# A hybrid decoder step on one core: peer_u handed over in a second layout, and the gates read four blocks at a time

## The chip, the cores and the metric

The kernel runs on one core of one Trainium2 chip. The number is the device time of one execution in microseconds. A core has five engines that work side by side and meet at semaphores: TensorE (PE), VectorE (DVE), ScalarE (ACT), GpSimd (POOL) and SyncE (SP, which here only issues transfers). Sixteen DMA engines move the data between memory, SBUF and back; one queue is fed by SP, another by GpSimd.

## What is computed

One decoder layer for 512 prompt tokens and 32 sample tokens, with a model dimension of 2048, in fp32. A pooling and gating mixer and a memory attention come first. The last sublayer, PEER, is what the change touches: every token picks 16 of 16384 experts in each of 8 heads, and each expert is one row of `peer_u` and one row of `peer_v`.

```python
def block(xb):
    q = (xb @ peer_wq).reshape(PEER_BLOCK, PEER_HEADS, 2, PEER_HALF)
    s = jnp.einsum('thpd,pkd->thpk', q, peer_subkeys).astype(jnp.float32)
    sv, si = lax.top_k(s, PEER_TOPK)
...
    fv, fi = lax.top_k(cand, PEER_TOPK)
    eidx = jnp.take_along_axis(cidx, fi, axis=-1)
    gate = jax.nn.softmax(fv, axis=-1).astype(xb.dtype)
    act = jax.nn.gelu(jnp.einsum('thkd,td->thk', peer_u[eidx], xb))
    return jnp.einsum('thk,thkd->td', gate * act, peer_v[eidx])
```

## The kernel before, in words

**Two ways through PEER.** 384 prompt tokens (N) go densely: their product with all 16384 rows of `u`, a GELU, the product with a mostly zero gate matrix, and the product with all rows of `v`. The other 128 prompt tokens and the 32 sample tokens go sparsely: GpSimd gathers their expert rows with 320 indirect transfers of 1 MB into seven buffers (`gbuf`), and VectorE does one "step" for each.

**Three passes of fp32r.** Each fp32 operand is split in a high half (a copy to fp32r on ScalarE) and a low half (the difference, on VectorE), and each product is made of three matmuls: high by high, high by low, low by high.

**The column stage.** The rows of `u` are cut in 128 blocks of 128 experts. One block is a "column" for PE: 16 chunks of the model dimension, three matmuls of 128x384 each, 48 in all, into a bank of `pl` (L1127). The model dimension must lie on partitions for it, and in memory a row of `u` lies along a partition. So during column b PE also transposes block b+1 from `u_raw`: after the second chunk of each four, four transposes (`turn_rows`, L1095) into a bank of `pp`. ScalarE copies the bank to `ut_hi` (`rows_hi`, L1418), VectorE makes `ut_lo` (`rows_lo`, L1838). `u_raw`, `ut_hi` and `ut_lo` have two slots. SP reloads half a slot of `u_raw` once PE has transposed it (`t_done`). After its column a block's GELU goes to `fg` (L1424).

**What runs beside the columns.** In the first 32 columns (PICK) VectorE and GpSimd pick the experts: `half_list` and `pick`, with calls of `next_rows` between the operations, which keep up the low halves of `u`. VectorE's instructions stand in one fixed order, so a call that waits holds the pick. The softmax's exponential stands on ScalarE between two columns. Then PE turns `ij` and `gw` to `ijt` (L1160), and 24 columns follow that also build the gate matrices (`gate_columns`): for every four tokens VectorE compares an iota with the picked indices (`one_hot`, L1886 and L1887), PE multiplies (L1104), ScalarE copies to `gs` (L1436), and GpSimd's queue stores to `g_scr`.

**Ahead and steady.** The gates are there only after these columns, so the GELUs of the first 60 blocks (AHEAD) are stored in `s_scr`. From block 60 on each column multiplies its own GELU by its gate (`gated`, L1931) and one of those stored (`ahead_gated`, L1936), and SP stores both to `p_scr`. SP's order in a steady column is: first half of `u_raw`, store of `sa`, store of `fg`, second half of `u_raw`, load of this block's gate `gt`, a wait until the store of `sa` has landed, loads of the next `sa` and its gate `ga`. A gate load reads 64 floats (256 bytes) at a time, 768 runs for a block. VectorE's gather steps start at column 62 (STEP_COL), three in two columns.

**The value stage.** 256 half blocks of `v` with their `p`, 24 matmuls each (L1186), again with high and low halves (L1490, L1493, L1940, L1944) and gather steps between.

Of the kernel before, what the change touches and what calls it, by code (L numbers as in the profile page):

```python
# [24 lines left out]
P = 128  # L25
# [25 lines left out]
PICK = 32  # L51
AHEAD = 60
STEP_COL = 62
STEP_M = 246
GELU_S = 43
# [21 lines left out]
def program(nc, a, o):  # L77
    ctx = ExitStack()
    with ctx:
# [400 lines left out]
        gt = at("gt", TMP, [P, 2, N])  # L480
        sa = at("sa", TMP + 3072, [P, 2, N])
        ga = at("ga", TMP + 9728, [P, 2, N])
# [3 lines left out]
        t_done, t_hi, t_lo = sem("t_done"), sem("t_hi"), sem("t_lo")  # L486
        u_done, ge_done, gm_done = sem("u_done"), sem("ge_done"), sem("gm_done")
        f_stored = [sem("f_stored0"), sem("f_stored1")]
        g_in, pa_stored = [[sem(f"{w}{s}") for s in range(2)] for w in ("g_in", "pa_stored")]
# [4 lines left out]
        def gates_in(b):  # L494
            n = (b - AHEAD) // 2 + 1
            return 48 * n if b < 2 * AHEAD else 16 * n + 32 * (AHEAD // 2)

# [11 lines left out]
        def acc_bank(c):  # L509

            k = c % 8
            return (pt[k] if k < 2 else pp[k // 2 - 1][:, k % 2] if k < 6 else pl[:, k % 2])[:, 0:N]
# [59 lines left out]
        def _(sp):  # L572
# [60 lines left out]
            uv = a["peer_u"][0].rearrange("(b p) d -> b p d", p=P)  # L633
            vv = a["peer_v"][0].rearrange("(b p) (s d) -> s b p d", p=P, s=2)
            gv = g_scr.rearrange("h p i t -> i p h t")

            def u_load(i, d, h, free=None):

                if free is not None:
                    sp.wait_ge(t_done, free)  # L640
                sp.dma_start(u_raw[:, d, h * HD:(h + 1) * HD], uv[i * 2 + d][:, h * HD:(h + 1) * HD])\
                    .then_inc(u_in[d][h], 16)

            def next_u(i, d, h):

                u_load(i + 1, d, h, i * 8 + (4 * d + 2 * (h + 1)))
# [5 lines left out]
            def p_store(i, d):  # L652
                sp.wait_ge(gm_done, i * 4 + (2 * d + 1 - 2 * AHEAD) if not isinstance(i, int) else gated_count(i * 2 + d))
                sp.dma_start(p_scr[i * 2 + d], fg[:, d, :]).then_inc(f_stored[d], 16)

            def g_load(i, d):
                sp.dma_start(gt[:, d, :].rearrange("p (h t) -> p h t", t=HALF), gv[i * 2 + d]).then_inc(g_in[d], 16)

            def ahead_load(i, d, first=False):
                if not first:  # L660
                    sp.wait_ge(pa_stored[d], i * 16)
                sp.dma_start(sa[:, d, :], s_scr[i * 2 + d]).then_inc(g_in[d], 16)
                sp.dma_start(ga[:, d, :].rearrange("p (h t) -> p h t", t=HALF), gv[i * 2 + d]).then_inc(g_in[d], 16)

            def ahead_store(i, d):
                sp.wait_ge(gm_done, i * 4 + (2 * d + 2))
                sp.dma_start(p_scr[i * 2 + d], sa[:, d, :]).then_inc(pa_stored[d], 16)
# [31 lines left out]
            def steady_body(i, d, first=False):  # L699
                b = i * 2 + d if isinstance(i, int) else None  # L700
                if b is None or b + 2 < NK:
                    next_u(i, d, 0)
# [4 lines left out]
                if b is None or AHEAD + 2 <= b < 2 * AHEAD + 2:  # L707
                    ahead_store(i - AHEAD // 2 - 1, d)
                if b is None or b >= AHEAD + 2:
                    p_store(i - 1, d)  # L710
                if b is None or b + 2 < NK:
                    next_u(i, d, 1)
                g_load(i, d)
                if b is None or b < 2 * AHEAD:
                    if b == AHEAD or b == AHEAD + 1:
                        sp.wait_ge(f_stored[d], 16 * AHEAD // 2)
                    ahead_load(i - AHEAD // 2, d, b is not None and b < AHEAD + 2)
            for d in range(2):
                steady_body(AHEAD // 2, d)
            with sp.Fori(AHEAD // 2 + 1, AHEAD) as i:  # L720
                for d in range(2):
                    steady_body(i, d)
            for b in range(2 * AHEAD, NK):
                if b == NK - 2:
                    for s in range(2):
                        sp.wait_ge(pa_stored[s], 16 * AHEAD // 2)
                    for d in range(4):
                        p_load(0, d)
                    sp.wait_ge(t_done, 4 * (NK - 1))
                    for d in range(2):  # L730
                        v_load(0, 0, d)
                steady_body(b // 2, b % 2)
            sp.wait_ge(t_done, 4 * NK)
            for d in range(2, 4):
                v_load(0, 0, d)
            for d in range(2):
                p_store(NK // 2 - 1, d)
# [29 lines left out]
        def _(pe):  # L767
# [317 lines left out]
            def turn_rows(i, d, g, dst, first=False):  # L1085

                if g % 2 == 0:
                    pe.wait_ge(u_in[d][g // 2], i * 16 + 16)
                if first:
                    if g >= 2:  # L1090
                        pe.wait_ge(t_lo, g - 1)
                else:
                    pe.wait_ge(t_lo, i * 8 + (4 * d + g - 3))
                for c in range(4):
                    last = turn(dst[:, c * P:(c + 1) * P], u_raw[:, d, (4 * g + c) * P:(4 * g + c + 1) * P], ident[:, :])  # L1095
                last.then_inc(t_done, 1)

# [1114 lines left out]
```

## Time and profile before

| What | Value |
|---|---|
| Median of 3 runs | 4282.88 us (4282.53 to 4288.63) |
| Profiled execution | 4279.69 us, span 4278.0 us |
| PE busy | 4077.9 us, 95% of the span |
| DVE busy | 2592.4 us, 61% |
| ACT busy | 1390.0 us, 32% |
| POOL busy | 714.2 us, 17% |
| Moved by DMA | 943.10 MB, mean 220 GB/s |
| Mean granted TensorE clock | 0.977 |

Busy times are averages over stages that differ: the projections up to about 1757 us, the column stage from there to 3165 us, the value stage to about 4238 us, then the last norms. Matmuls overlap in the pipe, so the mean duration of one is longer than the distance from one start to the next. A DMA share of 1 says that the sixteen engines had packets in flight all the time. What is named as idle or waiting on an engine costs time only where nothing else ends later.

### The profile page before, as it was taken

What the parts mean: (1) busy time and instruction counts of PE and PEld (TensorE: products, weight loads), DVE (VectorE), ACT (ScalarE), POOL (GpSimd) and SP (SyncE); (2) the same over time, 40 slices, a digit from 0 to 9 for tenths busy, and PEclk for the clock granted to TensorE, in tenths of its full rate; (3) what the DMA queues carried; (4) which work ended last, traced back from release to release, by engine and by line L of the source; (5) the groups of instructions that cost most, each with busy time, mean ns of one, the idle gap of its engine ahead of it and who ended that gap; (6) DMA issues with size and microseconds to landing.
All of it is one profiled execution on the core that took longest, in us unless ns stands there. A gap on an engine that the chain in (4) does not pass through costs nothing.

```text
span 4278.0 us, 69824 instructions
## 1 busy us (share of the span) xinstructions
PE 4077.9 (95%) x26191; PEld 3935.2 (92%) x26191; DVE 2592.4 (61%) x4092; ACT 1390.0 (32%) x1876; POOL 714.2 (17%) x514
## 2 busy tenths in 40 slices
PE   8998979979889979999999999999999999999996
PEld 6788969979849979999999999999999999999996
DVE  3324232351453266666477556666679899898896
ACT  3433221132442132222355422222233333333333
POOL 0000020020000030044100001111123333344430
PEclk9989989989999999999999999999999999999998
DMA  6542222213542212233344599999999999999994
GB/s 224 196 117 55 82 59 79 78 50 118 197 138 79 78 54 77 97 117 121 113 171 169 195 315 355 354 350 355 355 339 403 397 411 409 394 400 396 402 384 135
DMA packets 495289, 943.10 MB, mean 220 GB/s; under 512 B 126372, under 2 KB 375904, under 8 KB 443032
## 3 DMA queue, kind: packets, MB, share of 16 engines
q1 hardware_dynamic: 443552, 567.36, 39.8%
q0 software_dynamic: 51616, 374.19, 21.8%
q8 instruction: 68, 1.11, 0.1%
q14 instruction: 53, 0.43, 0.0%
HBM read 866.63 MB, written 73.56 MB: 220 GB/s over the span
## 4 chain that ended last, share of the span: by engine, by line
PE 91%; DVE 4%; DMA 2%; ACT 2%; DVEq 1%; issue 1%; POOL 0%; SPq 0%; ACTq 0%
PE pl L1127 25%; PE pp L197 24%; PE pp L1186 12%; PE pt L1186 6%; PE pl L1186 6%; PE pp L1095 5%; PE pt L1104 2%; PE pp L792 2%; PE pt L792 1%; PE pl L792 1%; PE pp L859 1%; DMA kv<-in_cache_mem_k 1%; DMA raw<-in_w_mk 1%; PE pl L821 1%; PE pt L823 1%; PE pl L1046 1%
## 5 line engine op out<-in xcount | busy, mean ns | idle before, releaser
L1127 PE MATMUL pl<-h_hi,ut_hi 128*128 128x384 f32 x2048 | 734.7, 359 | 0.6 <-ACT ijt L1465 0.6
L1127 PE MATMUL pl<-h_hi,ut_lo 128*128 128x384 f32 x2048 | 692.1, 338 | 0.0
L1127 PE MATMUL pl<-h_lo,ut_hi 128*128 128x384 f32 x2048 | 691.3, 338 | 0.0
L1838 DVE TENSOR_TENSOR ut_lo<-pp,ut_hi 128x512 fp32r<-128x512 f32 x508 | 350.2, 690 | 483.3 <-ACT ut_hi L1418 479.1
L1418 ACT ACTIVATE ut_hi<-pp 128x512 fp32r<-128x512 f32 x508 | 304.1, 599 | 820.6 <-PE pp L1095 763.4
L212 DVE TENSOR_TENSOR w_lo<-raw,w_hi 128x2048 fp32r<-128x2048 f32 x120 | 274.8, 2291 | 424.0 <-ACT w_hi L207 424.0
L1490 ACT ACTIVATE v_hi<-v_raw 128x1024 fp32r<-128x1024 f32 x256 | 271.9, 1062 | 682.6 <-PE pl L1186 438.3
L1940 DVE TENSOR_TENSOR v_lo<-v_raw,v_hi 128x1024 fp32r<-128x1024 f32 x256 | 313.2, 1223 | 123.3 <-ACT v_hi L1490 122.6
L1127 PEld LDWEIGHTS pl<-h_lo,ut_hi 128*128 128x128 f32 x2048 | 387.1, 189 | 0.0
L1127 PEld LDWEIGHTS pl<-h_hi,ut_hi 128*128 128x128 f32 x2048 | 386.2, 189 | 0.8 <-ACT ijt L1465 0.8
L1127 PEld LDWEIGHTS pl<-h_hi,ut_lo 128*128 128x128 f32 x2048 | 384.7, 188 | 0.0
L207 ACT ACTIVATE w_hi<-raw 128x2048 fp32r<-128x2048 f32 x120 | 229.4, 1911 | 418.9 <-PE pp L197 298.2
L197 PE MATMUL pp<-h_hi,w_hi 128*128 128x272 f32 x1664 | 350.9, 292 | 9.4 <-DVE w_lo L212 8.3
L197 PE MATMUL pp<-h_hi,w_lo 128*128 128x272 f32 x1664 | 347.9, 291 | 0.0
L197 PE MATMUL pp<-h_lo,w_hi 128*128 128x272 f32 x1664 | 346.6, 290 | 0.0
L1186 PE MATMUL pp<-p_hi,v_hi 128*128 128x384 f32 x1024 | 344.6, 336 | 0.0
L1186 PE MATMUL pp<-p_hi,v_lo 128*128 128x384 f32 x1024 | 343.8, 336 | 0.0
L1186 PE MATMUL pp<-p_lo,v_hi 128*128 128x384 f32 x1024 | 342.9, 335 | 0.0
L1095 PE MATMUL pp<-ident,u_raw 128*128 128x128 f32 x2032 | 304.4, 272 | 0.0
L2175 POOL DMA_INDIRECT gbuf<-in_peer_v,eix x128 | 242.6, 1895 | 355.6 <-DVE xr L1924 323.0
L1924 DVE SCALAR_TENSOR_TENSOR xr<-gbuf,wr,xr 128x2048 f32<-128x2048 f32 x128 | 300.4, 2347 | 0.1
L1920 DVE SCALAR_TENSOR_TENSOR gbuf<-gbuf,xr 128x2048 f32<-128x2048 f32 x128 | 292.2, 2283 | 0.0
(387 smaller groups left out, 8257.7 us busy)
## 6 DMA issues: line engine op xcount, KB each, us to landing
u_raw<-in_peer_u SPq DMA_DIRECT2D x256, 512.0 KB
v_raw<-in_peer_v SPq DMA_DIRECT2D x256, 512.0 KB
p_f<-p_scr SPq DMA_DIRECT2D x256, 192.0 KB
raw<-in_w_in SPq DMA_DIRECT2D x24, 1024.0 KB, 5.6
g_scr<-gs POOLq DMA_DIRECT2D x6, 4096.0 KB, 13.6
raw<-in_w_mk SPq DMA_DIRECT2D x16, 1024.0 KB, 4.9
raw<-in_w_mv SPq DMA_DIRECT2D x16, 1024.0 KB, 4.8
raw<-in_w_out SPq DMA_DIRECT2D x16, 1024.0 KB, 5.9
```

The lines of the kernel that those rows point to most:

```text
L197: last = nc.tensor.matmul(pp[s][:, b, 0:t1 - t0], w[:, s, k, :], x[:, k, t0:t1], start=(k == 0 and w is w_hi and x is x_hi), stop=(k == KC ...
L212: nc.vector.tensor_tensor(w_lo[:, s], raw[:, s], w_hi[:, s].bitcast(F32), ALU.subtract).then_inc(lo_ready, 1)
L1095: last = turn(dst[:, c * P:(c + 1) * P], u_raw[:, d, (4 * g + c) * P:(4 * g + c + 1) * P], ident[:, :])
L1127: last = mm(pl[:, d, 0:N], w[:, d, k, :], x[:, k, S:S + N], start=(k == 0 and w is ut_hi and x is h_hi), stop=(k == KC - 1 and w is ut_lo))
L1186: last = mm(acc_bank(c), w[:, d, c * P:(c + 1) * P], x[:, d, :], start=(b == 0 and w is v_hi and x is p_hi), stop=(b == NK - 1 and w is v_lo))
L1418: f(ut_hi[:, d, 4 * g:4 * g + 4, :], src.rearrange("p (c i) -> p c i", c=4), ACT.Copy).then_inc(t_hi, 1)
L1490: f(v_hi[:, d, :], v_raw[:, d, :], ACT.Copy).then_inc(hi_done, 1)
L1838: tt(ut_lo[:, d, 4 * g:4 * g + 4, :], src.rearrange("p (c i) -> p c i", c=4), ut_hi[:, d, 4 * g:4 * g + 4, :].bitcast(F32), ALU.subtract). ...
L1920: ins = stt(row, row, 1.0, x, ALU.mult, ALU.mult, accum_out=s[:, k:k + 1])
L1924: ins = stt(x, row, w[:, k:k + 1], x, ALU.mult, ALU.add)
L1940: tt(v_lo[:, m % 4, :], v_raw[:, m % 4, :], v_hi[:, m % 4, :].bitcast(F32), ALU.subtract).then_inc(lo_done, 1)
L2175: g.indirect_dma_start(gbuf[n % NG_BUF][:, :], None, rows, bass.IndirectOffsetOnAxis(ix, 0))\
```

## The change

1. `peer_u` is handed over a second time, laid out as [block, model dimension within a chunk, chunk, expert]. The dense path loads its blocks from that; the gathers keep the old one. `turn_rows` is gone, and `u_raw` holds what was in the banks.
2. `rows_hi` and `rows_lo` read `u_raw` in SBUF, half a block (128x1024) at a time, two pieces a block instead of four. SP reloads half a slot when the low half has been made (`t_lo`).
3. Gates are read for four blocks at once (`gate_fours`), 1024 bytes at a time, in two buffers each for the current and the stored blocks (`g4`, `a4`).
4. `one_hot` makes three operations of 128x4x128 with broadcast operands instead of eight of 128x128, and works one group ahead of PE.
5. PICK is 28 instead of 32, AHEAD 56 instead of 60, STEP_COL 58 instead of 62, GELU_S 46 instead of 43. The steps' pace is 5 in 4 columns from 58 and 2 a column from 112, 99 in all before the value stage, as many as before.
6. The columns' accumulators lie in `pp[0]`, and the value stage takes its banks in another order. The last select-scores product moves into column 0, the first block's halves ahead of the last panel's evacuation on ScalarE.
7. On VectorE one score list less stands before the first halves.

```diff
-PICK = 32
-AHEAD = 60
-STEP_COL = 62
+PICK = 28
+AHEAD = 56
+STEP_COL = 58
...
             def u_load(i, d, h, free=None):

                 if free is not None:
-                    sp.wait_ge(t_done, free)
+                    sp.wait_ge(t_lo, free)
...
+            def gate_fours(k, both=True):
+
+                for dst, q in ((g4, k + AHEAD // 4),) + (((a4, k),) if both else ()):
+                    sp.dma_start(dst[k % 2][:, :, :, :], gv[q]).then_inc(g4_in[k % 2], 16)
...
+            def ahead_steady(j, d, b=None):
+
+                s = d % 2
+                sp.wait_ge(t_lo, j * 16 + (2 * d + 1))
+                sp.dma_start(u_raw[:, s, 0:HD], uv[j * 8 + (d + 2)][:, 0:HD]).then_inc(u_in[s][0], 16)
                 if b == AHEAD:
                     s_store(AHEAD // 2 - 1, 1)
-                    for s in range(2):
-                        sp.wait_ge(g_stored[s], 16 * ND)
+                    for x in range(2):
+                        sp.wait_ge(g_stored[x], 16 * ND)
+                    for k in range(2):
+                        gate_fours(k)
                 if b is None or b >= AHEAD + 2:
+                    sp.wait_ge(gm_done, j * 16 + (2 * (d - AHEAD) - 2))
+                    sp.dma_start(p_scr[j * 8 + (d - AHEAD - 2)], sa[:, s, :]).then_inc(pa_stored[s], 16)
+                    sp.wait_ge(gm_done, j * 16 + (2 * (d - AHEAD) - 3))
+                    sp.dma_start(p_scr[j * 8 + (d - 2)], fg[:, s, :]).then_inc(f_stored[s], 16)
+                sp.wait_ge(t_lo, j * 16 + (2 * d + 2))
+                sp.dma_start(u_raw[:, s, HD:D], uv[j * 8 + (d + 2)][:, HD:D]).then_inc(u_in[s][1], 16)
+                if b is None or b >= AHEAD + 2:
+                    sp.wait_ge(pa_stored[s], j * 64 + (16 * (d // 2 - AHEAD // 2)))
...
+                sp.dma_start(sa[:, s, :], s_scr[j * 8 + (d - AHEAD)]).then_inc(s_in[s], 16)
+                if d % 4 == 1 and (b is None or b > AHEAD + 1):
+
+                    x = (d // 4 + 1) % 2
+                    sp.dma_start(g4[x][:, :, :, :], gv[j * 2 + (d // 4 + 1)]).then_inc(g4_in[x], 16)
+                    if b is None or b < 2 * AHEAD - 4:
+                        sp.dma_start(a4[x][:, :, :, :], gv[j * 2 + (d // 4 + 1 - AHEAD // 4)]).then_inc(g4_in[x], 16)
...
                 for k in range(KC):
-                    if k % 4 == 0:
-                        pe.wait_ge(t_lo, i * 8 + (4 * d + k // 4 + 1))
+                    if k % 8 == 0:
+                        pe.wait_ge(t_lo, i * 4 + (2 * d + k // 8 + 1))
                     for w, x in ((ut_hi, h_hi), (ut_hi, h_lo), (ut_lo, h_hi)):
-                        last = mm(pl[:, d, 0:N], w[:, d, k, :], x[:, k, S:S + N],
+                        last = mm(pp[0][:, d, 0:N], w[:, d, k, :], x[:, k, S:S + N],
                                   start=(k == 0 and w is ut_hi and x is h_hi), stop=(k == KC - 1 and w is ut_lo))
                     if k == KC - 1:
                         last.then_inc(u_done, 1)
-                    if k % 4 == 1:
-                        if more:
-                            turn_rows(i + d, 1 - d, k // 4, turn_bank(k // 4))
-                        if gate is not None:
-                            gate_matrix(group(gate, k // 4)[0], k // 4 % 2)
+                    if start and d == 0 and k == 7:
+                        select_scores(NPANEL - 1, 1)
+                    if gate is not None and k % 4 == 1:
+                        gate_matrix(group(gate, k // 4)[0], k // 4 % 2)
...
+            def rows_hi(i, d, h, used=None):
+
+                act.wait_ge(u_in[d][h], i * 16 + 16)
                 if used is not None:
                     act.wait_ge(u_done, used)
-                f(ut_hi[:, d, 4 * g:4 * g + 4, :], src.rearrange("p (c i) -> p c i", c=4), ACT.Copy).then_inc(t_hi, 1)
+                f(ut_hi[:, d, 8 * h:8 * h + 8, :], u_raw[:, d, h * HD:(h + 1) * HD].rearrange("p (c i) -> p c i", c=8),
+                  ACT.Copy).then_inc(t_hi, 1)
...
+            def rows_lo(i, d, h):
+
+                dve.wait_ge(t_hi, i * 4 + (2 * d + h + 1))
+                tt(ut_lo[:, d, 8 * h:8 * h + 8, :], u_raw[:, d, h * HD:(h + 1) * HD].rearrange("p (c i) -> p c i", c=8),
+                   ut_hi[:, d, 8 * h:8 * h + 8, :].bitcast(F32), ALU.subtract).then_inc(t_lo, 1)
...
+                k_all = iota_k[:, :].rearrange("p (x k) -> p x k", x=1).to_broadcast([P, 4, P])
+                tt(oh[:, s, 1, :, :], k_all, of(0), ALU.is_equal)
+                tt(oh[:, s, 0, :, :], k_all, of(1), ALU.is_equal)
+                dve.drain()
+                tt(oh[:, s, 1, :, :], oh[:, s, 1, :, :], of(2), ALU.mult).then_inc(oh_ready, 1)
...
             for b in range(AHEAD, NK):
                 more = b + 1 < NK
-                upto = max(0, b + 1 - STEP_COL) * 3 // 2
...
+                upto = max(0, b + 1 - STEP_COL) * 5 // 4 + max(0, b + 1 - 2 * AHEAD) * 3 // 4
+                if more:
+                    rows_lo((b + 1) // 2, (b + 1) % 2, 0)
+                if b > AHEAD:
+                    gated(b - 1)
+                if AHEAD < b <= 2 * AHEAD:
+                    ahead_gated(b - AHEAD - 1)
+                if more:
+                    rows_lo((b + 1) // 2, (b + 1) % 2, 1)
+                else:
+                    for m in range(2):
+                        v_split(m)
+                        p_split(m)
+                while done[0] < upto:
+                    step()
```

## Rows read from the trace of the kernel before

**Rows 1.** The page's chain that ended last, shares of the span by line.
```profile
PE pl L1127 25%; PE pp L197 24%; PE pp L1186 12%; PE pt L1186 6%; PE pl L1186 6%; PE pp L1095 5%; PE pt L1104 2%; PE pp L792 2%; PE pt L792 1%; PE pl L792 1%; PE pp L859 1%; DMA kv<-in_cache_mem_k 1%; DMA raw<-in_w_mk 1%; PE pl L821 1%; PE pt L823 1%; PE pl L1046 1%
```
**Rows 2.** The page's groups: shapes, count | busy us, mean ns | idle before, releaser.
```profile
L1838 DVE TENSOR_TENSOR ut_lo<-pp,ut_hi 128x512 fp32r<-128x512 f32 x508 | 350.2, 690 | 483.3 <-ACT ut_hi L1418 479.1
L1418 ACT ACTIVATE ut_hi<-pp 128x512 fp32r<-128x512 f32 x508 | 304.1, 599 | 820.6 <-PE pp L1095 763.4
...
L1095 PE MATMUL pp<-ident,u_raw 128*128 128x128 f32 x2032 | 304.4, 272 | 0.0
```
**Rows 3.** Windows: us, busy of PE, PEld, DVE, ACT, POOL, PEclk, DMA share, GB/s.
```profile
1757.00:2095.00 338.00, 336.43 (x2147) 330.04 (x2145) 205.63 (x576) 105.64 (x183) 110.64 (x54) 1.00 0.37 123
...
2431.00:3165.00 734.00, 734.00 (x4611) 723.37 (x4610) 468.66 (x614) 209.90 (x363) 101.20 (x106) 1.00 0.99 343
...
3190.00:3700.00 510.00, 508.23 (x2922) 507.46 (x2920) 457.93 (x430) 182.99 (x249) 175.06 (x111) 1.00 1.02 404
```
**Rows 4.** Timeline of ScalarE, two GELUs two columns apart: start, us, what.
```profile
2800.26 0.49 ACT L1424 ACTIVATE fg<-pl 128x384 f32<-128x384 f32 x1 [0.45 <-PE pl L1127]
...
2820.63 0.49 ACT L1424 ACTIVATE fg<-pl 128x384 f32<-128x384 f32 x1 [0.45 <-PE pl L1127]
```
**Rows 5.** Timeline of PE, first product of the last column and first value product.
```profile
3156.59 0.34 PE L1127 MATMUL pl<-h_hi,ut_hi 128*128 128x384 f32 x1
...
3165.02 0.34 PE L1186 MATMUL pt<-p_hi,v_hi 128*128 128x384 f32 x1
```
**Rows 6.** Timeline of PE in a column that builds gate matrices.
```profile
2134.80 0.60 PE L1095 MATMUL pp<-ident,u_raw 128*128 128x128 f32 x4
2135.23 1.10 PE L1104 MATMUL pt<-oh 128*128 128x128 f32 x8
2136.09 0.42 PE L1127 MATMUL pl<-h_hi,ut_hi 128*128 128x384 f32 x1
```
**Rows 7.** The page's groups of the value stage and of the gather steps.
```profile
L1490 ACT ACTIVATE v_hi<-v_raw 128x1024 fp32r<-128x1024 f32 x256 | 271.9, 1062 | 682.6 <-PE pl L1186 438.3
L1940 DVE TENSOR_TENSOR v_lo<-v_raw,v_hi 128x1024 fp32r<-128x1024 f32 x256 | 313.2, 1223 | 123.3 <-ACT v_hi L1490 122.6
...
L1924 DVE SCALAR_TENSOR_TENSOR xr<-gbuf,wr,xr 128x2048 f32<-128x2048 f32 x128 | 300.4, 2347 | 0.1
```
**Rows 8.** Timeline of VectorE: softmax of the gates, one gate product.
```profile
2073.18 0.82 DVE L1861 TENSOR_TENSOR gw<-gw,sums 128x640 f32<-128x640 f32 x1
2075.12 0.82 DVE L1864 TENSOR_REDUCE sums<-gw 128x40 f32<-128x640 f32 x1 [1.12 <-ACT gw L1460]
...
2599.79 0.54 DVE L1931 TENSOR_TENSOR fg<-fg,gt 128x384 f32<-128x384 f32 x1
```
**Rows 9.** Timelines of VectorE, GpSimd and PE where the pick ends.
```profile
2037.08 2.81 DVE L1816 TENSOR_TENSOR eq<-iota,ab_f 128x2560 f32<-128x2560 f32 x1
...
2051.26 0.47 POOL L2136 TENSOR_TENSOR ij<-eq 128x160 f32<-128x160 f32 x1
...
2094.15 0.55 PE L1160 MATMUL pt<-ident,ij 128*128 128x128 f32 x3 [1.27 <-DVE sums L1878]
...
2097.54 0.69 PE L1127 MATMUL pl<-h_hi,ut_hi 128*128 128x384 f32 x1 [0.58 <-ACT ijt L1465]
```
**Rows 10.** Groups by form of 1810 to 1900 us.
```profile
L1789 DVE MATCH_REPLACE8 cand<-gw,cand 128x256 f32<-128x256 f32 x15 | 6.0, 410 | 0.0
```
**Rows 11.** DMA of 2600 to 2980 us, rates in 40 slices of 9.5 us.
```profile
GB/s 394 327 367 359 345 373 323 376 319 392 318 390 315 388 321 381 347 348 371 340 373 323 380 321 397 311 394 306 390 329 372 353 344 371 342 371 331 379 314 399
DMA packets 92892, 134.83 MB, mean 355 GB/s; under 512 B 61915, under 2 KB 76145, under 8 KB 85617
```
**Rows 12.** Waits of SP's queue, 2600 to 3100 us: us in total, times, longest.
```profile
SPq L662 <- DMA p_scr<-sa: 87.1, 35, 3.8
```
**Rows 13.** Timelines of SP and ScalarE in the value stage.
```profile
3182.85 0.29 SPq L677 DMA_DIRECT2D p_f<-p_scr  x1
...
3190.64 1.06 ACT L1490 ACTIVATE v_hi<-v_raw 128x1024 fp32r<-128x1024 f32 x1 [5.42 <-DMA p_f<-p_scr]
```

More of the change, by code:

```diff
@@ new lines, in _ @@
+            for d in range(8):
+                ahead_steady(AHEAD // 8, d, AHEAD + d)
+            with sp.Fori(AHEAD // 8 + 1, AHEAD // 4 - 1) as j:
+                for d in range(8):
+                    ahead_steady(j, d)
+            for d in range(4):
+                ahead_steady(AHEAD // 4 - 1, d, 2 * AHEAD - 8 + d)
+            for b in range(2 * AHEAD - 4, 2 * AHEAD):
+                ahead_steady(AHEAD // 4 - 1, b % 8, b)
+            for b in range(2 * AHEAD, NK):
+                s = b % 2
+                if b + 2 < NK:
+                    next_u(b // 2, s, 0)
+                if b < 2 * AHEAD + 2:
+                    sp.wait_ge(gm_done, 2 * (b - AHEAD) - 2)
+                    sp.dma_start(p_scr[b - AHEAD - 2], sa[:, s, :]).then_inc(pa_stored[s], 16)
@@ L724, in _ @@
                 if b == NK - 2:
-                    for s in range(2):
-                        sp.wait_ge(pa_stored[s], 16 * AHEAD // 2)
+                    for x in range(2):
+                        sp.wait_ge(pa_stored[x], 16 * AHEAD // 2)
                     for d in range(4):
                         p_load(0, d)
-                    sp.wait_ge(t_done, 4 * (NK - 1))
+                    sp.wait_ge(t_lo, 2 * (NK - 1))
                     for d in range(2):
                         v_load(0, 0, d)
-                steady_body(b // 2, b % 2)
@@ L733, in _ @@
-            sp.wait_ge(t_done, 4 * NK)
+                p_store(b - 2)
+                if b + 2 < NK:
+                    next_u(b // 2, s, 1)
+                if b % 4 == 1 and b + 4 < NK:
+                    gate_fours((b - AHEAD) // 4 + 1, False)
+            sp.wait_ge(t_lo, 2 * NK)
             for d in range(2, 4):
@@ L1083, in _ @@
                     select_scores(i * 2 + (WQ0 + d - 1), (d + 1) % 2)
[L1085 to L1096, printed above, removed]
             def gate_matrix(n, s):
@@ L1423, in gelu, with column @@
                     act.wait_ge(f_stored[d], i * 16)
-                f(fg[:, d, :], pl[:, d, 0:N], ACT.Gelu_apprx_tanh).then_inc(ge_done, 1)
-            def column(i, d, gate=None, more=True):
+                f(fg[:, d, :], pp[0][:, d, 0:N], ACT.Gelu_apprx_tanh).then_inc(ge_done, 1)
+            def column(i, d, gate=None):
                 first = isinstance(i, int) and i == 0 and d == 0
                 for g in range(4):
-                    if more:
-                        rows_hi(i + d, 1 - d, g, turn_bank(g), None if first or g else i * 2 + d)
+                    if g % 2 == 0:
+                        if first:
+                            act.wait_ge(panel_done, NPANEL)
+                        rows_hi(i + d, 1 - d, g // 2, None if first else i * 2 + d)
+                    if first and g == 1:
+                        scores_out(15)
                     if gate is not None:
```

185 lines of the change are left out of this document (68 added, 117 removed).

## The prediction

> **What bounds the kernel now.** Read the chain that ended last first: its longest entries are all TensorE's, 25% in the products of `ut` with `h` (L1127) and 5% in the transposes of `u` (L1095) [rows 1]. The groups give the counts: 2032 transposes (16 more stand before the first column), with two off-path companions, the high half on ScalarE (L1418) and the low half on VectorE (L1838), both of which wait longer than they work [rows 2]. The windows say what else is full: in the column stage PE is busy for 336 of the first 338 us and for all of the last 734, at full granted clock, and in the last part the DMA share is 0.99 as well [rows 3]. So two things are full there, PE and, from about 2450 us, the DMA engines. The reader has to hold both: time taken from PE is only won if the DMA engines can deliver the same bytes sooner.
>
> **What a transpose costs on the path.** Its mean of 272 ns overlaps its neighbours, so I take distances between starts. Two GELUs later in the steady part are 20.37 us apart, 10.19 us a column [rows 4]. The last column has no transposes: its 48 products start at 3156.59 and the next work at 3165.02, 8.43 us, 0.1756 us each [rows 5]. The difference, 1.76 us a column, is the price of 16 transposes, 0.44 us for each group of four. In the columns that also build gate matrices, four transposes start at 2134.80 and the gate matrix at 2135.23, 0.43 us [rows 6]: the same.
>
> **Term 1: no transposes.** 127 columns carry them: 127 x 1.75 = 222 us. The chain's own entry, 5% of 4278 us, gives 214, rounded as it is [rows 1]. Block 0's 16 transposes stand before the first product, at the same price 1.8 us. The select-scores product beside them moves into column 0 and costs what it did. Sum: -224 us.
>
> **Term 2: the halves are made from SBUF in pieces of 1024.** Per column ScalarE did 4 x 0.60 and will do 2 x 1.06 (as `v_hi`, same shape and source); VectorE did 4 x 0.69 and will do 2 x 1.22 (as `v_lo`) [rows 2, 7]. Both drop. They lie behind PE: block b+1 is made while column b runs. If that cover were gone the column would start at least 1.06 + 1.22 = 2.3 us late. In the columns from 58 on VectorE has 2.44 + 2 x 0.55 (gates) + 1.25 x 2.35 (gather steps) = 6.5 us [rows 7, 8] of work in 8.43; from 112 on 2.44 + 0.55 + 2 x 2.35 = 7.7. It stays below PE, tightly at the end, where a half may be late by a step and still be ready, since it is due only 8.4 us after its column's start. Cost 0.
>
> **Term 3: one-hot matrices in three wide operations.** No row has this form. Its neighbours on VectorE: 384 elements took 0.54, 640 with a broadcast operand 0.82, 2560 with two broadcast operands 2.81 us [rows 8, 9]. For 512 that is 0.68, so 2.0 us for three. The upper end is `v_lo` of 1024, 1.22 each, 3.7 us. PE's period for a group becomes 12 x 0.1756 + 0.86 for the gate matrix, 3.0 us [rows 5, 6]; VectorE needs 2.0 + 0.61 for its half of a `ut_lo`, 2.6. I take the lower end, because 384 and 640 enclose 512. It would bind from 0.8 us an operation on. Cost 0, upper value at 0.9 us: (2.7 + 0.07 + 0.61 - 3.0) x 96 groups = 36 us; at the upper end itself, 3.7 + 0.61 - 3.0 = 1.3 us a group, 125 us.
>
> **Term 4: the pick of experts gets 28 columns instead of 32.** Now the last `eq` on VectorE starts at 2037.08, GpSimd ends its reductions at 2051.7, and PE turns `ij` at 2094.15: some 40 us of slack, filled with columns [rows 9]. In the new order the last pick begins with half-blocks 51, 52, 53; the 52nd (block 26) needs column 24 finished. From there, with the rows' durations: GELU and high half 1.7, low half 1.2, the rest of the top-16, fifteen small operations of about 0.41 like the replacement, with one more half 7.1 [rows 10], index work and `eq` 3.6, so `eq` ends 13.6 us after column 25 starts, the subtraction at 14.5. ScalarE stands at the exponential until 16.6 (the reduction now starts 1.94 us after the subtraction did [rows 8]) and only then makes block 27's high halves; VectorE does reduction, reciprocal and product (some 2.2, three operations of the sizes of these rows) and then the low half: 20.1. Column 27 is due at 16.9. So PE waits about 3.3 us, and pays perhaps 1 us of lower clock behind it, as after the present pause, where the first product is 0.69 us long instead of 0.34 [rows 5, 9]. GpSimd, 11.7 us behind the end of `eq`, ends at 25.3, before column 27 does (28.5), so the second pause keeps its present length. +4 us; 0 if the pick runs ahead, 12 if the chain slips by a column.
>
> **Term 5: DMA.** Per column from 58 to 111 the queues carry u 1.05 MB, two stores and one load of 0.197, two gate loads of 0.197 (now 0.79 MB once in four columns) and 1.25 gathers of 1.05: 3.34 MB. The gathers' pace per us is kept (1.5 in 10.19 before, 1.25 in 8.43). In 8.43 us that is 397 GB/s; from 112 on, 3.54 MB, 420 GB/s for 16 columns, part of which the seven gather buffers give from stock. Now the same stage runs at 343 to 355 GB/s with the share at 0.99, which looks full. But 61915 of its 92892 packets are under 512 B, the slices reach 390 to 399 GB/s in columns with two steps, and SP waits only 87.1 / 35 = 2.5 us for a store to land; the value stage keeps 404 GB/s with PE busy for 508 of 510 us [rows 3, 11, 12]. The gates' packets go from 256 to 1024 B, a quarter of the number. So I take cost 0, lower end 0. Upper end: if 355 were the ceiling, a column takes 3.34/0.355 = 9.41 us, +0.98 x 54 = 53, and 3.54/0.355 = 9.97, +1.54 x 16 = 25: +78 us. At the first gated column two quads of both gates (3.1 MB, 8 us at 400 GB/s) stand in SP's queue before the second half of block 58, which is due some 18 us later: cost 0, at most 8.
>
> One page has a say here. The Trainium skill, DMA: Bandwidth & Descriptors, Specifications, lists about 358 GB/s of HBM bandwidth per core. By that the sum would be 9.33 and 9.89 us a column, +72 us, about 4132. The trace of this single core does not agree: 404 GB/s over 510 us [rows 3].
>
> **Queues past which work moves.** SP waits now on `t_lo`, that is on VectorE, to reload `u_raw`. Behind that wait stand the stores of `sa` and `fg` and the load of `sa`, and for these VectorE's gate products and ScalarE's GELU wait. A half is freed about 2.5 and 5 us into a column and read two columns later, so 12 to 14 us remain for the transfer. The longest landing I can work out is in the value stage, issued 3182.85, used 3190.64: 7.8 us for 0.7 MB [rows 13].
>
> **The sum.** -224 + 0 + 0 + 4 + 0 = -220 us. The profiled execution took 4279.69 us (span 4278.0), 3.2 below the median of 4282.88. From its own time: 4059.7; from the median 4063. I predict 4062 us.
>
> **Rivals.** (a) DMA becomes the bound from column 58: for it the share of 0.99 and the 397 GB/s wanted; against it the rows of term 5. At a ceiling of 385 GB/s: 8.68 and 9.19 us, +0.25 x 54 + 0.76 x 16 = 26, 4088 us; at 355, 4140. (b) VectorE bounds the gate columns: 4062 + 36 = 4098; the interpolation speaks against it. (c) The pick's end slips by a column more: 4070. (d) Slower than before: `u_raw` has two slots, now released by VectorE and refilled over SP, so PE runs at the loop's pace: issue 0.35, landing L, 1.06, 1.22, over two columns. To lose 224 us over the 104 plain columns a column must take 8.43 + 2.15 = 10.6 us, the loop 21.2, so L of 18 us or more; the time would be 4284 and up. The longest seen is 7.8.
>
> **How the numbers follow.** PE stays the bound everywhere (own range 4050 to 4076, (c) included): 0.70. (a) 0.18, two thirds of it below 4110. (b) 0.08, mostly below 4110. (d) 0.02. A rest of 0.02 for something between the present time and 4140. 4050 to 4110 then holds 0.68 + 0.12 + 0.06, some 0.85. A difference of 0.2% (8.6 us) is what a measurement can tell here: faster 0.97, same 0.01, slower 0.02.
>
> **What would show it.** GELUs 8.43 us apart in plain columns and 12.1 in gate columns, no idle on PE between; DMA near 400 GB/s from column 58; PE idle of 2 to 5 us just before the turning of `ij`; SP's wait for `pa_stored` longer than 2.5 us. Wrong if PE waits for `ut_lo` and behind it ScalarE for `u_raw` (a), or if one-hot operations take over 0.8 us (b), or if the products without transposes between are not 0.1756 us apart.

## The result and the profile after

| kernel | median us | runs | ratio to before, 95% interval |
|---|---|---|---|
| before | 4284.93 | 4 | |
| changed | 4134.44 (4119.98 to 4144.23) | 4 | 0.9645 [0.9614, 0.9677] |

The change makes the kernel 150 us faster. The prediction said 4062, with a range of 4050 to 4110: the direction was right, a third of the gain is missing. The profiled execution took 4130.32 us (span 4128.6), 70.6 us over the 4059.7 that the sum gave against its own time.

Distances between GELUs, which [rows 4] gave for the kernel before, place the loss. The kernel after, timeline of ScalarE, first in the plain columns before block 56, then further on:

```profile
2316.44 0.49 ACT L1422 ACTIVATE fg<-pp 128x384 f32<-128x384 f32 x1 [6.04 <-PE pp L1134]
2324.87 0.49 ACT L1422 ACTIVATE fg<-pp 128x384 f32<-128x384 f32 x1 [6.04 <-PE pp L1134]
...
2591.39 0.49 ACT L1422 ACTIVATE fg<-pp 128x384 f32<-128x384 f32 x1 [5.98 <-DMA p_scr<-fg]
2609.59 0.49 ACT L1422 ACTIVATE fg<-pp 128x384 f32<-128x384 f32 x1 [15.78 <-DMA p_scr<-fg]
2615.30 0.49 ACT L1422 ACTIVATE fg<-pp 128x384 f32<-128x384 f32 x1 [3.34 <-DMA p_scr<-fg]
2623.17 0.49 ACT L1422 ACTIVATE fg<-pp 128x384 f32<-128x384 f32 x1 [5.44 <-PE pp L1134]
2631.59 0.49 ACT L1422 ACTIVATE fg<-pp 128x384 f32<-128x384 f32 x1 [6.04 <-PE pp L1134]
```

8.43 us apart, as predicted, while GELU waits for PE. Further on the rows are 18.2, 5.71, 7.87 and 8.42 us apart, 40.2 for four columns that need 33.7, and what the GELU waits for is the landing of a store. From GELU 56 to GELU 111 the trace has 523.6 us; 55 x 8.43 is 463.7. Windows of the kernel after, in the columns of [rows 3]:

```profile
2460.00:2780.00 320.00, 288.66 (x1569) 286.45 (x1568) 199.07 (x213) 78.96 (x99) 60.41 (x40) 0.94 0.93 340
2890.00:3000.00 110.00, 110.00 (x629) 110.00 (x628) 94.35 (x92) 31.53 (x40) 47.87 (x27) 1.00 1.02 413
```

In the long stretch PE is busy for 289 of 320 us, but the DMA share is 0.93 as well, at 340 GB/s: neither is full. In the last columns, where more is wanted (420 GB/s by the prediction's count), the DMA engines bring 413 and PE never stops. So the first stretch waits for something that is neither bandwidth nor PE. Waits of SP's queue and of ScalarE in these 320 us, total us, times and longest (before, in 500 us, [rows 12]: 87.1, 35, 3.8):

```profile
SPq L714 <- DMA p_scr<-sa: 204.4, 33, 16.9
ACT fg L1422 <- DMA p_scr<-fg: 168.0, 21, 18.7
```

And the chain of waits from 2540 to 2600 us, start and length of each piece:

```profile
2543.13 6.28 DMA p_scr<-sa
...
2550.12 0.38 SPq L718
2550.55 0.05 SPq L720
...
2552.49 15.23 DMA p_scr<-sa
...
2569.01 4.38 DMA p_scr<-sa
...
2575.18 5.38 DMA p_scr<-sa
...
2581.94 8.88 DMA p_scr<-sa
...
2593.29 15.75 DMA p_scr<-sa
```

The chain is SP's own program: store `sa`, wait until it has landed, load `sa` into the same slot, load u, store again. L718 and L720 issue the two gate loads of four blocks, 768 KB each. The two 192 KB stores just behind such loads land after 15.2 and 15.8 us, the four others after 4.4 to 8.9. Over columns 56 to 111 of this trace the 13 stores behind gate loads took 7.7 to 19.0 us (median 13.6), the 43 others took 4.2 to 10.6 (median 5.7). The other two losses, at the pick's end and in the value stage, come below.

### The profile page after: what moved, and what is told of

It is laid out like the page before. It is cut to its first block, busy times and chain, and to the rows that moved or that the text cites. A ratio compares the mean times of both kernels' runs of the same rounds, so it can differ in the third digit from the quotient of the medians.

```text
span 4128.6 us, 62540 instructions
## 1 busy us (share of the span) xinstructions
PE 3873.2 (94%) x24143; PEld 3747.4 (91%) x24143; DVE 2592.3 (63%) x3356; ACT 1327.0 (32%) x1620; POOL 806.3 (20%) x514
## 4 chain that ended last, share of the span: by engine, by line
PE 65%; DMA 16%; DVE 12%; ACT 3%; issue 2%; SPq 2%; DVEq 1%; POOL 0%; ACTq 0%
PE pp L197 25%; PE pp L1134 15%; DMA p_scr<-sa 9%; PE pp L1184 6%; DMA p_f<-p_scr 5%; PE pt L1184 3%; PE pl L1184 3%; DVE gbuf L1926 3%; PE pt L1108 2%; PE pp L809 2%; DVE v_lo L1949 2%; DVE xs_r L1930 1%; PE pt L809 1%; DVE p_lo L1953 1%; PE pl L809 1%
## 5 line engine op out<-in xcount | busy, mean ns | idle before, releaser
L1134 PE MATMUL pp<-h_hi,ut_hi 128*128 128x384 f32 x2048 | 713.1, 348 | 51.8 <-DVE ut_lo L1832 51.2
L1134 PE MATMUL pp<-h_lo,ut_hi 128*128 128x384 f32 x2048 | 698.1, 341 | 0.0
L1134 PE MATMUL pp<-h_hi,ut_lo 128*128 128x384 f32 x2048 | 696.1, 340 | 0.0
L1832 DVE TENSOR_TENSOR ut_lo<-u_raw,ut_hi 128x1024 fp32r<-128x1024 f32 x256 | 333.0, 1304 | 285.5 <-ACT ut_hi L1415 283.7
L1134 PEld LDWEIGHTS pp<-h_hi,ut_hi 128*128 128x128 f32 x2048 | 392.0, 191 | 56.2 <-DVE ut_lo L1832 55.0
L1134 PEld LDWEIGHTS pp<-h_lo,ut_hi 128*128 128x128 f32 x2048 | 391.8, 191 | 0.0
L1134 PEld LDWEIGHTS pp<-h_hi,ut_lo 128*128 128x128 f32 x2048 | 390.9, 191 | 0.0
L2184 POOL DMA_INDIRECT gbuf<-in_peer_u,eix x128 | 203.3, 1588 | 504.3 <-DVE gbuf L1926 492.6
L197 PEld LDWEIGHTS pp<-h_hi,w_hi 128*128 128x128 f32 x1664 | 265.4, 191 | 13.9 <-issue 11.1
## 6 DMA issues: line engine op xcount, KB each, us to landing
g_scr<-gs POOLq DMA_DIRECT2D x6, 4096.0 KB, 13.3
```

Of the source, the lines that this page charges most:

```text
L197: last = nc.tensor.matmul(pp[s][:, b, 0:t1 - t0], w[:, s, k, :], x[:, k, t0:t1], start=(k == 0 and w is w_hi and x is x_hi), stop=(k == KC ...
L1134: last = mm(pp[0][:, d, 0:N], w[:, d, k, :], x[:, k, S:S + N], start=(k == 0 and w is ut_hi and x is h_hi), stop=(k == KC - 1 and w is ut_lo))
L1832: tt(ut_lo[:, d, 8 * h:8 * h + 8, :], u_raw[:, d, h * HD:(h + 1) * HD].rearrange("p (c i) -> p c i", c=8), ut_hi[:, d, 8 * h:8 * h + 8, :] ...
L2184: g.indirect_dma_start(gbuf[n % NG_BUF][:, :], None, rows, bass.IndirectOffsetOnAxis(ix, 0))\
```

## The experiments

Each kernel's time is the median of its runs (four, five for e11 and e12), and its ratio is to the kernel before on the same chip. Where the text speaks of a stage, it goes by one trace of each kernel. "Columns 56 to 111" is the time from GELU 56 to GELU 111 in its trace.

**e1_spread: the gate loads in thirds.**

```diff
-                if d % 4 == 1 and (b is None or b > AHEAD + 1):
+                if d % 4 >= 1 and (b is None or b > AHEAD + 3):
+                    x, m = (d // 4 + 1) % 2, d % 4 - 1
+                    gate_part(g4[x], j * 2 + (d // 4 + 1), m, x)
```

> Edit: from the second group of four on, the two gate loads of a group of four (0.79 MB each) are issued in three pieces of a third each, one piece of each in the three columns after the first of a group, in place of both whole in one column. Bytes, packets of 1 KB, slots and waits stay. Burst theory (a 197 KB store that stands behind 1.57 MB lands after 15 to 16 us, and SP's wait for that store holds up all that follows): no store stands behind more than 0.52 MB, columns 56 to 111 take 480 to 500 us in place of 532, the time is 4085 to 4105. Bandwidth rival (355 GB/s is what the core gets in this stage): the same bytes take the same time, 525 to 540 us, 4125 to 4140.

4165.78 us, 0.9713 [0.9697, 0.9729], columns 56 to 111 in 542.5 us: 31 us slower than the changed kernel, against both theories. The burst theory had counted one large load as the harm. GELU's waits for the fg store rose (from 168.0 to 230.3 us in 2460 to 2780) and no longer fall on one column in four: with a piece ahead of the stores in three columns of four, I read it as nearly every turn of SP's chain being somewhat longer; e5 below tests that. The equal bytes did not take equal time either, so this speaks against a bandwidth limit too: 329 GB/s at share 0.93.

**e2_slots: three slots for sa.**

```diff
-        sa = at("sa", TMP + 9728, [P, 2, N])
+        sa = at("sa", TMP + 9472, [P, 3, N])
...
-                    sp.wait_ge(pa_stored[s], j * 64 + (16 * (d // 2 - AHEAD // 2)))
+                if q >= 3:
+                    sp.wait_ge(pa_stored[q % 3], pa_base[q % 3] + 16 * (q // 3))
```

> Edit: three slots for sa in place of two, so that SP waits, before it loads sa, for the landing of a store it issued a column earlier and not in the same column; the whole gate loads of four blocks stay as they are. (SP's loop over these columns is written out, and a4's second slot lies 1280 bytes further.) SP-order theory (the loss comes from SP standing at the wait for the sa store while u loads and stores queue behind it in program order): SP's wait for the landing falls from 328 us to under 60, and the time to 4080 to 4105. Burst-alone theory (what is late is the fg store and the u loads that stand behind 1.57 MB in the DMA queues, whatever SP does): 4115 to 4135. Bandwidth rival: 4125 to 4140.

4087.00 us, 0.9531 [0.9506, 0.9555]: 47 us of the missing 70 come back by moving one wait, with the same loads in the same places. (SP's loop is also written out here. Its turn costs some 0.5 us once in eight columns in the chain above, so that is not what the 47 us were.) Columns 56 to 111 take 480.7 us. SP's wait for the landing in 2460 to 2780 us falls from 204.4 us to 45.2. From 2420 to 2620 us PE is busy throughout, at 390 GB/s; after that single stalls are not made up any more, the longest pieces of whose chain are the other store and a u load behind the gate loads:

```profile
2594.97 16.27 DMA u_raw<-in_peer_ut
2629.86 15.49 DMA p_scr<-fg
```

**e3_slices: gates one block at a time.**

```diff
-            gv = g_scr.rearrange("h p (q i) t -> q p h i t", i=4)
+            gv1 = g_scr.rearrange("h p i t -> i p h t")
+            def gate_slice(dst, d, b):
+                sp.dma_start(dst[d // 4 % 2][:, :, d % 4, :], gv1[b]).then_inc(g4_in[d % 8], 16)
```

> Edit: the transposes stay removed, but the gates are read for one block at a time, 197 KB in runs of 256 bytes, as in the kernel before, each two columns ahead of its use, into the same slots. Burst and SP-order theories: nothing stands behind more than one 0.39 MB pair, the stage runs at 8.5 to 8.9 us a column, the time is 4080 to 4100, so the reading by fours cost some 40 us. Rival (packets under 512 bytes are what held the kernel before to 348 GB/s): 3.34 MB take 9.6 us a column, +64 us over 8.43, 4130 to 4150, so reading by fours was what the removal of the transposes needed.

4184.12 us, 0.9746 [0.9730, 0.9763], the slowest of all and above both ranges; 564.9 us for the 55 columns. With the rest of the change in place, reading by fours gains 43 us by the ratios, 50 by the medians; it is not the cost that I had suspected. Windows and packets of this kernel:

```profile
2460.00:2780.00 320.00, 276.37 (x1483) 265.50 (x1481) 187.64 (x201) 73.79 (x93) 51.28 (x38) 0.97 0.96 320
DMA packets 75721, 102.47 MB, mean 320 GB/s; under 512 B 51450, under 2 KB 62997, under 8 KB 70726
```

SP's waits are shorter than in the changed kernel (140.6 us, longest 7.7) and the DMA share higher (0.96), at a lower rate: part of this loss is the small packets, part still the chain. One number on record narrows it: e1, on the same chip, also spreads the gate loads over the columns but keeps runs of 1 KB, and is 18 us faster (4165.78). The rest was not taken apart.

**e5_slots_spread: three slots and thirds.** The edits of e1 and e2 together.

> Edit: both of the first two edits, three slots for sa and the gate loads of four blocks spread over three columns. Spreading alone made it slower (4166), the third slot alone faster (4087). Chain theory (each landing that SP or a GELU waits for is what costs, and spreading put a gate piece in front of a store in three columns of four in place of one): with SP's wait gone, what is left is the landing of the fg store behind at most 0.52 MB, which is under 10 us; 4065 to 4090, no slower than with the third slot alone. Rival (the DMA engines take longer for the same bytes once the pieces stand between other traffic): slower than with whole loads here too, 4095 to 4125.

4072.61 us, 0.9492 [0.9472, 0.9511]. Columns 56 to 111 take 464.5 us, 8.44 each: the whole loss of this stage is gone. Its window, SP's wait, and the chain of waits from 2480 to 2700 us, which is one piece:

```profile
2460.00:2780.00 320.00, 320.00 (x1825) 320.00 (x1824) 231.28 (x249) 91.22 (x115) 69.93 (x48) 1.00 1.03 396
```

```profile
SPq L716 <- DMA p_scr<-sa: 0.7, 2, 0.5
```

```profile
2479.87 220.15 PE pp L1126 x1254
```

396 GB/s is what the prediction said such columns want (3.34 MB in 8.43 us), and it is delivered. The edit that cost 31 us on two slots is worth 14 us on three. By the whole times these 14 us are barely clear of the noise (e2's interval and e5's touch), but the traces place them: 480.7 us for the 55 columns against 464.5. Here how the load is cut matters through what waits behind it.

**e6_actq and e7_actq_slots: the gate loads on ScalarE's queue.**

```diff
-                    sp.dma_start(dst[k % 2][:, :, :, :], gv[q]).then_inc(g4_in[k % 2], 16)
+                    act.dma_start(dst[k % 2][:, :, :, :], gv[q]).then_inc(g4_in[k % 2], 16)
```

> Edit: the changed kernel with two slots for sa, and the gate loads of four blocks whole, but issued on ScalarE's queue, after the GELU of the column, in place of SP's. SP's own queue then carries u, the stores and sa alone. Same-queue theory (the stores land late, after 15 to 16 us, because 1.57 MB stand before them in the same queue): they land in 4 to 7 us, SP's wait for the sa store and the GELU's for the fg store go, 4065 to 4095. Engine-share theory (any 1.57 MB that the 16 DMA engines carry delay a store by as much, on whichever queue it stands): landings stay at 9 to 16 us, 4115 to 4140.

> Edit: the gate loads on ScalarE's queue and three slots for sa. Same-queue theory: columns 56 to 111 at 8.43 to 8.5 us each, the time 4065 to 4080. Bandwidth rival in its mildest form (397 GB/s is a little more than the core gets with these packets, and the gather buffers only lend for some 30 columns): the stalls of columns 89 to 107 that are seen with three slots stay, 4080 to 4095.

e6 took 4126.34 us, 0.9629 [0.9604, 0.9654], 502.3 us for the 55 columns; e7 4087.92, 0.9536 [0.9513, 0.9558], 471.0 us. With its own queue the burst still delays a store. From e6's chain of waits:

```profile
2474.79 14.25 DMA p_scr<-sa
2490.85 5.10 DMA p_scr<-sa
...
2511.89 12.10 DMA p_scr<-sa
2525.27 4.40 DMA p_scr<-sa
...
2545.85 13.05 DMA p_scr<-sa
```

In the chain from 2400 to 2760 us the store just after gate loads takes 11.4 to 14.3 us, where the changed kernel has 11.6 to 19.0, and the others 4.3 to 10.4 us. So the engine-share theory holds for most of it: what is in flight on the sixteen engines delays the store, whichever queue it came from. The Trainium skill, DMA: Bandwidth & Descriptors, section Queues, rings and completion order, says that a DMA engine goes round the queues that have work, packet by packet. By that a store would hardly feel a load on the other queue; the trace agrees in the direction alone, a median of 12.1 us against 15.5. With three slots the stage loses 7 us, where e5 loses 1, and 5 us more go before GELU 56, where ScalarE issues the first gate loads. e7's time lies in the range of the mild bandwidth rival, but e5, with the same bytes at 8.44 us a column, speaks against that rival.

**e4_poolwait: VectorE waits for GpSimd at the pick's end.**

```diff
+            dve.wait_ge(pool_step, PICK_STEPS * PH)
             dve.drain()
             gw4 = gw[:, :, :].rearrange("p t (h k) -> p (t h) k", k=TOPK)
```

> Edit: at the pick's end VectorE waits until GpSimd has ended all its reductions before it starts the softmax over gw (it did so by itself in the kernel before). Shared-port theory (VectorE's operations with two operands in SBUF are stretched while GpSimd works on SBUF): the subtraction on gw falls from 6.05 to 0.8 to 0.9 us, the ut_lo behind it are 1.22 each, and GpSimd's last group of three is 5.3 to 6 us in place of 7.1; since all of it is later, PE waits as long or longer and the time is 4130 to 4150. Rival (the stretch comes from the DMA traffic or from ScalarE): the durations stay at 6 and 1.8 to 3 us.

4138.32 us, 0.9656 [0.9627, 0.9686], the same time as the changed kernel. What it shows is in the durations. First the changed kernel, VectorE and GpSimd:

```profile
1992.59 6.05 DVE L1863 TENSOR_TENSOR gw<-gw,sums 128x640 f32<-128x640 f32 x1
...
2001.98 6.74 DVE L1832 TENSOR_TENSOR ut_lo<-u_raw,ut_hi 128x1024 fp32r<-128x1024 f32 x4
```

```profile
1992.37 5.59 POOL L2141 TENSOR_TENSOR eq<-eq,sif 128x2560 f32<-128x2560 f32 x1 [4.79 <-DVE eq L1816]
1998.04 7.06 POOL L2144 TENSOR_TENSOR eq<-eq 128x1280 f32<-128x1280 f32 x3
```

Then e4, the same operations:

```profile
2007.89 0.82 DVE L1864 TENSOR_TENSOR gw<-gw,sums 128x640 f32<-128x640 f32 x1
...
2011.63 2.35 DVE L1832 TENSOR_TENSOR ut_lo<-u_raw,ut_hi 128x1024 fp32r<-128x1024 f32 x2
```

```profile
1996.09 5.58 POOL L2142 TENSOR_TENSOR eq<-eq,sif 128x2560 f32<-128x2560 f32 x1 [4.81 <-DVE eq L1816]
2001.75 5.24 POOL L2145 TENSOR_TENSOR eq<-eq 128x1280 f32<-128x1280 f32 x3
```

With GpSimd idle the subtraction takes 0.82 us again, as in [rows 8], and GpSimd alone 5.24 for what took 7.06. Each engine can slow the other, but not evenly: GpSimd's operation beside the subtraction took 5.59 us, and 5.58 alone. In the changed kernel that operation ends at 1997.96 and the subtraction 0.7 us later, so VectorE stood for nearly the whole of it. The Trainium skill, GPSIMD Engine Reference, section Specifications, says that GpSimd shares its SBUF interfaces with VectorE, with contention for VectorE instructions with two SBUF inputs; the trace agrees, 6.05 against 0.82 us. The time did not move, because VectorE's 11.7 us of waiting for GpSimd took the place of what the stretch had cost; PE waits 16.3 us for `ut_lo` there, 11.7 in the changed kernel.

**e8_pick30: 30 columns for the pick.** `PICK = 30` in place of 28.

> Edit: the changed kernel with 30 columns for the pick in place of 28, so that two more columns, 16.9 us, lie between the last pick and the turning of ij, and the gate matrices end two columns before they are read again. Late-pick theory: VectorE reaches the subtraction on gw only when GpSimd has ended or nearly so, the three long distances of columns 25 to 27 (18.1, 12.9 and 16.5 us) become 8.43 each but for the pause before ij; minus 8 to 16 us. Against it: the last store of the gate matrices (4.2 MB) is now two columns nearer to its first reader, where SP waits for it with u loads behind: plus 0 to 10 us. Sum 4118 to 4136. Rival (the pause only moves to the new end of the pick): 4130 to 4142.

4140.79 us, 0.9663 [0.9635, 0.9690], no gain. The pick's end did get shorter: the distances there were 18.1, 12.9 and 16.5 us (8.43, 8.43 and 12.0 without a pause), 18.6 us too many; now 11.4, 12.0 and 16.5, 11.0 too many. But the subtraction still met GpSimd (3.54 us), and the first gated column now takes 23.3 us in place of 12.0: 11 us lost where 8 were won. SP does not wait for the last store of the gate matrices, which landed at 2329.3 us, 4.5 us before SP issued the gate loads. What takes longer is issuing them. The third of the four, in the changed kernel and in e8:

```profile
2343.70 5.12 SPq L660 DMA_DIRECT2D g<-g_scr  x1
```

```profile
2334.84 12.10 SPq L660 DMA_DIRECT2D g<-g_scr  x1
```

GpSimd starts seven gathers of 1 MB only when the last gate matrices are stored. They now begin 4 us before the gate loads, where it was 20, and the second half of block 58 is issued behind the gate loads, 12 us after GELU 56 in place of 1.5. That the gathers are what the loads meet is read from these times and was not tested.

**e9_rows_first: the halves before the softmax** (on e5).

```diff
+            for d in range(2):
+                column(PICK // 2 - 1, d)
             act.wait_ge(g_sub, 1)
             f(gw[:, :, :], gw[:, :, :], ACT.Exp).then_inc(g_exp, 1)
-            for d in range(2):
-                column(PICK // 2 - 1, d)
...
             while turned[0] < 2 * (PICK - 1):
                 next_rows(1)
-
+            next_rows(4, 2 * (PICK + 1))
```

> Edit, on top of the kernel with three slots for sa and spread gate loads (4073): at the pick's end VectorE makes the low halves of blocks 27 and 28 before it starts the softmax over gw, and ScalarE's exponential stands behind the column 27 in place of before column 26. Order theory (PE's wait of 11.7 us for ut_lo comes from the exponential, behind which the high halves of blocks 27 and 28 stand, and which itself waits for a subtraction stretched to 6 us): columns 26 and 27 start 8.43 us apart, the softmax moves into column 27 and ends some 5 us after it, and of the 14 us lost there 8 to 12 come back: 4060 to 4066. Rival (GpSimd's reductions are what ij waits for, so the same time is only spent in front of the turning of ij): 4069 to 4077.

4069.02 us, 0.9498 [0.9483, 0.9512], not told apart from e5. The rival was right. PE's wait for `ut_lo` fell from 11.7 to 2.7 us, and 7.8 us of waiting stand in front of `ij` instead. The order was not the cause; the same stretch now falls on the halves, which take 1.22 us each when GpSimd is idle:

```profile
1989.36 14.20 DVE L1824 TENSOR_TENSOR ut_lo<-u_raw,ut_hi 128x1024 fp32r<-128x1024 f32 x4
```

**e10_fewer_steps and e12_hold: gather steps and the value stage.** The first diff is e10's, on e5; the second e12's, on e9. e11 is e9 and e10 together.

```diff
-GELU_0 = 18
+GELU_0 = 20
...
-                upto = max(0, b + 1 - STEP_COL) * 5 // 4 + max(0, b + 1 - 2 * AHEAD) * 3 // 4
+                upto = max(0, b + 1 - STEP_COL) * 5 // 4
```

```diff
-                while done[0] < min(NSTEP, base + (m + 1) * (NSTEP - base) // STEP_M):
+                n = min(m, NK - 7) if m < NK + 4 else m
+                early = 6 * (n + 1) // (NK - 6) if m < NK + 4 else 0
+                while done[0] < min(NSTEP, base + (n + 1) * (NSTEP - base) // STEP_M + early):
```

> Edit, on the same kernel: no additional gather steps in columns 112 to 127, so that VectorE has 1.25 steps a column there as before them, and 12 steps more are left to the value stage. (ScalarE's second GELU for the gathers stands 8 value blocks later.) Theory (the value stage is 7 to 11 us longer than in the kernel before because VectorE, with 2 steps in 8.43 us where it had 1.5 in 10.2, arrives late with v_lo and p_lo, and PE, clocked down after the pause, pays again): PE's waits for p_lo fall from 5.7 us to about 2, columns 119 to 126 are 8.43 throughout, minus 3 to 6 us: 4066 to 4070. Rival (12 more steps in the value stage make VectorE the bound there): 4075 to 4090.

> Edit: both edits together with three slots and spread gate loads. If their gains add, 4054 to 4063; if the pick's end only shifts its wait, 4066 to 4072. My prediction on record said 4062, with 4 us for the pick's end.

> Edit, on top of three slots, spread gate loads and the reordered pick's end (4069): in the value stage no gather steps stand on VectorE between value product 122 and the eight additions to r at product 131; six of them are done earlier, spread over the first half. Theory (PE's second pause, 5 us in the changed kernel and 1.6 before, comes from VectorE reaching the additions late, with its steps in front; with 12 more steps there the wait was 12.5 us): the wait for r falls from 3.4 to under 1.5 us, and the low clock behind it goes too, 4063 to 4068. Rival (the six steps only crowd the first half, and p_lo is late there): 4069 to 4076.

e10 took 4081.80 us, 0.9522 [0.9508, 0.9537], e11 4082.70, 0.9522 [0.9509, 0.9535], e12 4079.03, 0.9512 [0.9499, 0.9525]. By the medians they are 9, 14 and 10 us slower than what they were built on, with intervals that overlap a little; e11 and e12 lie above every range given for them. The traces place the loss in the value stage: 1127.7 us from GELU 127 to the end for e10 (e5 1124.0), 1132.2 for e11 and 1128.6 for e12 (e9 1119.5). PE's waits in the value stage, for the changed kernel, e10 and e12:

```profile
PE pt L1184 <- DVE r L1957: 5.3, 1, 5.3
PE pt L1184 <- DVE p_lo L1953: 3.7, 2, 2.4
```

```profile
PE pt L1176 <- DVE r L1949: 12.5, 1, 12.5
...
PE pt L1176 <- DVE p_lo L1945: 1.7, 3, 0.8
```

```profile
PE pt L1176 <- DVE p_lo L1944: 13.3, 11, 4.7
```

Twelve more steps in the value stage make the wait at the additions to `r` 12.5 us; no steps in front of them make it vanish, and six more steps ahead of it bring 13.3 us of waits for `p_lo`. In both directions the pause follows VectorE's steps, and neither edit found a free place for them.

## Why the prediction was wrong, step by step

- **Term 1 held.** Plain columns are 8.43 us apart and gate columns 12.0 (predicted 12.1). From GELU 0 to GELU 24 the trace went from 249.4 to 208.0 us, 41.4 for 24 columns, 42.0 predicted.
- **Terms 2 and 3 held** in the plain and gate columns: PE waits for no half there and hardly for a one-hot matrix (0.8 us once), whose operations take 0.68 to 0.69 us, as estimated.
- **Term 5 failed, and with it the paragraph on the queues; this is the step that made the prediction wrong.** Its first half, that the DMA engines would deliver 397 GB/s, is right: e5 runs at 396 with PE full. The failure is "cost 0" for everything else about the transfers. I priced the gate loads of four blocks at the first gated column alone (8 us at most; it cost 3.5, and the next column gave 2.5 back) and not for the groups after it, where a store stands behind 1.57 MB. And I had read SP's wait for the landing as 2.5 us of harmless idling, expected only that it would grow, took 7.8 us for the longest landing (stores behind gate loads took up to 19.0), and did not ask how far the wait can grow before SP itself is late: each column has one such wait in a serial program, with u's loads and the other store behind it. Measured: +59.9 us in 55 columns; e2 takes 43 of it away by moving the wait, e5 59.
- **The 358 GB/s came close for another reason.** By this figure of the Trainium skill, DMA: Bandwidth & Descriptors, section Specifications, the sum would have been 4132, and the changed kernel took 4134. e5, with the same bytes, ran at 396 GB/s and 4073: that limit does not bind this single core, and the nearness was chance.
- **Term 4 was mis-sized.** The pauses around the pick's end were 6.3 us before (20.2 us to the first gate column, where 13.9 is normal) and are 18.6 now: 12 us more where 4 were taken. I had taken VectorE's and GpSimd's durations from stretches in which they did not overlap; GpSimd needed 14.1 us behind `eq`, not 11.7, and the subtraction 6.05, not 0.82. The upper value given, 12, came out.
- **Not foreseen: the value stage**, 1120.2 us after GELU 127 in place of 1112.8. The size is one trace's: e1 to e9, whose edits leave the value stage as it is, have 1116.6 to 1128.9 us there, all above 1112.8. The same 99 steps lie before it, but columns are shorter, so that VectorE enters it late; e10 and e12 show the dependence on the steps. PE's waits for `p_lo` and `r` grew from 3.4 to 9.0 us, 5.6 of the 7.4; the other 1.8 I put down to the lower clock that follows a pause, which is argued and not shown.

The sum: 4059.7 + 59.9 (columns 56 to 111) + 12.3 - 4 (pick) + 7.4 (value stage) makes 4135.3. Two things go against it: the columns began 2.4 us earlier than predicted, which lies within the 14 us by which that time varies between kernels that are equal up to there (1765.3 to 1779.3), and a gate column lost 1.93 us and not 1.75, 4.3 us for 24. That gives 4128.6; measured 4130.3.

Of the rivals, (a) has the right stage and nearly the right time, 4140 at a ceiling of 355, with the wrong mechanism. (d) has the right kind of mechanism, SP's loop as the pace, but on `u_raw` and at a landing of 18 us, where I had seen 7.8; landings of 15 to 19 us did come, on the stores. "SP's wait for `pa_stored` longer than 2.5 us" stood in the text as a sign that all goes well; it was the sign of the loss.

The best version, e5 or e9 (4072.61 and 4069.02), beats the changed kernel by 1.5%: the ratios to before are 0.9492 and 0.9498 against 0.9645, with intervals that do not meet.

## What to carry to other kernels

When one engine issues loads and stores and also waits for its own stores, write down its program for one turn and add the landings: in this kernel that sum, not the bytes, set how short the turn could be. A wait that the profile shows as short and harmless before a speedup is the first to be checked against the new, shorter turn, with the landing time it gets behind the largest transfer in flight. Give a buffer that is stored and reloaded one slot more before you judge how its neighbours should be cut: the same cut cost 31 us with two slots and gave 14 with three.

## What the runs showed of the hardware

- A 192 KB store of `sa` landed in 4.2 to 10.6 us in the changed kernel's steady columns, and in 7.7 to 19.0 us (mostly 11.6 and more) when gate loads had been issued just before it on its queue; with these on another queue (e6) it still took 11.4 to 14.3 us.
- This core moved 396 GB/s over 320 us (e5) and 413 over 110 us (the changed kernel), with stores, loads of 1 KB to 4 KB runs and gathers mixed. With gates in runs of 256 bytes (e3) it was 320 GB/s at DMA share 0.96, in a kernel that SP's waits still slowed.
- VectorE and GpSimd working on SBUF at the same time: 128x640 with two SBUF operands 6.05 us in place of 0.82, 128x1024 up to 6.7 (e9) in place of 1.22, a copy of 128x40 5.53 us (e8) in place of 0.20, and GpSimd's three of 128x1280 7.06 in place of 5.24.
- The changed kernel's four runs lie 24 us apart and e5's 8. That is no rule for programs paced by landings: e1's, paced by them too, lie 6 us apart.
